# The order of a closing head group's transposes in a Mamba scan, and its reciprocal root by way of a logarithm

## The chip, the cores and the metric

One Trainium2 chip, one core. The metric is the device time of one execution in microseconds (us). The engines are PE (TensorE), DVE (VectorE), ACT (ScalarE), POOL (GpSimd) and SP (SyncE, which issues the transfers).

## The reference

Two transformer-like blocks over 256 tokens of width 1024, in fp32. The first mixes an RWKV-7 and a retention branch and a convolutional feed-forward; the second is a Mamba-2 layer, a per-layer embedding, sliding-window attention and another embedding. The change touches the Mamba-2 layer alone, whose end is a grouped norm and a product:

```python
y = ssd_chunked(xs, dt, a, bm, cm)
y = y + d_skip[:, None] * xs
y = y.reshape(b, s, D_INNER) * silu(z)
yg = y.reshape(b, s, SSM_GROUPS, D_INNER // SSM_GROUPS)          # 4 groups of 512
yg = yg * lax.rsqrt(jnp.mean(yg * yg, axis=-1, keepdims=True) + EPS)
y = yg.reshape(b, s, D_INNER) * gnorm_w
return y @ out_w
```

## The kernel before

Every engine runs one program in order, and the engines meet by semaphores. A product in fp32 precision is three TensorE products of rounded parts: an upper part, made by ACT, and a lower part (the remainder), made by DVE. Weights come in units of 1 MB; for each unit ACT makes the upper part (helper `split_to`, L1358) and DVE then the lower part (its own `split_to`, L1925). Which unit is split in which step is written out by hand (`SPLIT`).

The scan runs over 16 steps z: four head groups g, in each two chunks n of 128 tokens, in each two halves hf. For a step PE spreads the running sums of the decay (`spread`, L928, one PSUM bank of two, fed by a mask that POOL makes), ACT takes their exponentials (`exps_of`, L1723), DVE weighs them (`weigh`, L2509), and after two halves PE forms the chunk's product (`diagonal`, L440/441). At z%4==2 PE also forms the part carried over from the first chunk (`carried`, L942).

A group closes in the four steps behind it. DVE joins and gates its rows (L2534 to L2546, `gated` L2516/2518), ACT squares and sums them (`group_squares`, L1701) and takes the root (`group_root`, L1706), and at z%4==1 DVE takes the reciprocal (L2550) and scales the rows (`group_scale`, L2553). At z%4==2 PE transposes the scaled rows, four blocks for each of the two token tiles (`group_turns`, which calls `turns`, L429); both tiles go to PSUM bank 7, one after the other. ACT copies each with its norm weight (`group_upper`, L1714) and DVE makes the remainder and frees the bank (`group_lower`, L2561); on DVE the order there is lower part of tile 0, join of the group that runs (L2534, which also frees the bank for `carried`), lower part of tile 1.

Behind the waits for data, PE has one fill in each step: up to z=6 a quarter of a gate product (`z_piece`), from z=8 on a slice of the layer's output product (`out_tile`), each of twelve products (L445 to L447); z=7 has none. At z=4 and z=6 ACT also takes the Tanh of gate rows (`z_tanh`, L1659), which DVE multiplies in (`gate_rows`, L2528). Behind the scan PE goes through the rest of the output product, with group 3's transposes in between, and the embedding begins: ACT prepares a Sqrt (`root_table`, L1389), sums the squares of the rows (L1399) and takes their root, and PE transposes the scaled rows.

ACT needs a table for each function that it looks up; where another table is needed, a load (ACT_TABLE_LOAD) stands ahead of the instruction, under its line. The program does not write these loads: the build places them.

Of the kernel before, what the change touches and what calls it, by code (L numbers as in the profile page):

```python
# [24 lines left out]
ACT = mybir.ActivationFunctionType  # L25
# [132 lines left out]
def build(nc, io, out, where, ncols):  # L158
    ctx = ExitStack()
    with ctx:  # L160
# [5 lines left out]
        def sem(name):  # L166
            if name not in sems:
                sems[name] = ctx.enter_context(nc.semaphore(name))
            return sems[name]
# [22 lines left out]
        def const(name):  # L192
            a, n = where[name]
            return consts[:, a:a + n]
# [14 lines left out]
        def sm(at, *shape):  # L209
            n = int(np.prod(shape))  # L210
            v = small[:, at:at + n]
            if len(shape) == 2:
                v = v.rearrange("p (a b) -> p a b", a=shape[0])
            if len(shape) == 3:
                v = v.rearrange("p (a b c) -> p a b c", a=shape[0], b=shape[1])
            return v
# [73 lines left out]
        mean, var, rs8 = sm(8, 2, 32), sm(72, 2, 32), sm(136, 2, 32)  # L290
# [14 lines left out]
        eps6 = sm(1364, 1)  # L305
# [63 lines left out]
        def take(pe, key, bank):  # L369
            if uses[bank]:  # L370
                pe.wait_ge(psum_emptied[bank], uses[bank])
            uses[bank] += 1
            use_of[key] = (bank, uses[bank])
            return PS[bank]

        def fill(ins, key):
            ins.then_inc(psum_full[use_of[key][0]], 1)

        def full(eng, key):
            bank, n = use_of[key]  # L380
            eng.wait_ge(psum_full[bank], n)
            return PS[bank]
# [38 lines left out]
        def _(pe):  # L421
            mm = pe.matmul

            def turns(key, bank, ins):

                ps = take(pe, key, bank)
                for j, a in enumerate(ins):
                    m, n = a.shape
                    last = pe.transpose(ps[0:n, j * P:j * P + m], a, ident[0:m, 0:m])  # L429
                fill(last, key)  # L430
# [438 lines left out]
            def z_piece(j, half, i, ready=False, between=None):  # L869
                if half == 0:  # L870
                    z_banks[j, i] = take(pe, z_keys(j)[i], 2 * (j % 2) + i)
                w = unit(f"z{j}.{half}")
                for k in range(4):
                    if between and k == 2:
                        between()
                    if ready:
                        xT_ready(2, 8 * i + 4 * half + k + 1)
                    last = mm3(z_banks[j, i][:, :], both(xT, every, 4 * half + k, slice(i * P, i * P + P)),
                               both(w, every, k, every), half + k == 0, half == 1 and k == 3)
                if half:  # L880
                    fill(last, z_keys(j)[i])
                if i:
                    used(f"z{j}.{half}", *((last,) if half == 0 else (None, z_keys(j)[1])))
# [38 lines left out]
            def spread(z):  # L922

                g, n, hf = STEPS[z]
                pe.wait_ge(sem("later_steps"), z + 1)
                ps = take(pe, ("bc", z), 4 + z % 2)
                for e in range(4):
                    last = mm(ps[:, P * e:P * e + P], later[:, z % 2, e, :], const("incl"), start=True, stop=True)  # L928
                fill(last, ("bc", z))

            def diagonal(g, n):
                pe.wait_ge(sem("wT_ready"), 4 * g + 2 * n + 2)
                ps = take(pe, ("yd", g, n), 6 + n)
                for e in range(8):
                    hd = 8 * g + e
                    last = halves(ps, slice(64 * e, 64 * e + 64), wT[:, n, e, :], xd[:, n, 64 * hd:64 * hd + 64], True, True)
                fill(last, ("yd", g, n))

            def carried(g):
                emptied(pe, ("sst", g))  # L940
                ps = take(pe, ("yo", g), 6)
                fill(mm(ps[:, :], xbc[:, 20 + g, P:2 * P], ss0[:, g, :], start=True, stop=True), ("yo", g))  # L942

            def group_turns(g, i):
                pe.wait_ge(sem("yg_rows"), 2 * g + i + 1)
                turns(("gT", g, i), 7, [xs[:, i, 512 * g + P * j:512 * g + P * j + P] for j in range(4)])
# [3 lines left out]
            def out_tile(t, tiles=(0, 1)):  # L950
                g = t // 4
                w = unit(f"so{t // 2}")
                for i in tiles:
                    if t == 0:
                        for f in range(2):
                            out_banks[i, f] = take(pe, ("so", i, f), 2 * i + f)
                    pe.wait_ge(sem("ygT_ready"), 2 * g + i + 1)
                    for f in range(2):
                        last = mm3(out_banks[i, f][:, :], both(ygT[g % 2], every, t % 4, slice(i * P, i * P + P)),
                                   both(w, every, t % 2, slice(512 * f, 512 * f + 512)), t == 0, t == 15)  # L960
                        if t == 15:
                            fill(last, ("so", i, f))
                if 1 in tiles:
                    if t == 15:
                        used("so7", key=("so", 1, 1))
                    elif t % 2:
                        used(f"so{t // 2}", last)
# [22 lines left out]
            pe.wait_ge(sem("xd_ready"), 3)  # L990
            GATES = [(j, half, i) for j in (2, 3) for half in range(2) for i in range(2)][1:]
            for z, (g, n, hf) in enumerate(STEPS):
                if z % 4 == 2 and g:
                    group_turns(g - 1, 0)
                if z < 7:
                    z_piece(*GATES[z])
                if z >= 8:
                    out_tile(z - 8)
                if z % 4 == 2 and g:
                    group_turns(g - 1, 1)  # L1000
                if z + 2 < 16:
                    spread(z + 2)
                if hf:
                    diagonal(g, n)
                if z % 4 == 2:
                    carried(g)
# [324 lines left out]
        def _(act):  # L1331
# [8 lines left out]
            A = act.activation  # L1340
# [313 lines left out]
            def z_tanh(j):  # L1654


                for i in range(2):
                    ps = full(act, ("z", j, i))
                    A(zrow[:, i, 512 * j:512 * j + 512], ps[:, :], ACT.Tanh, scale=0.5).then_inc(sem("z_tanh"), 1)  # L1659
# [39 lines left out]
            def group_squares(g, i):  # L1699
                act.wait_ge(sem("yz_ready"), 2 * g + i + 1)  # L1700
                A(xd[:, i, 512 * g:512 * g + 512], xs[:, i, 512 * g:512 * g + 512], ACT.Square,  # L1701
                  accum_out=mean[:, i, g:g + 1]).then_inc(sem("yg_sq"), 1)

            def group_root(g):
                act.wait_ge(sem("yg_sq"), 2 * g + 2)
                A(var[:, :, g], mean[:, :, g], ACT.Sqrt, scale=1.0 / 512, bias=eps6).then_inc(sem("yg_root"), 1)  # L1706

            def group_upper(g, i):
                if g >= 2 and i == 0:
# [16 lines left out]
            for z, (g, n, hf) in enumerate(STEPS):  # L1726
                if z < 15:
                    exps_of(z + 1)
                if z == 4:
                    z_tanh(2)  # L1730
                if z in SPLIT:
                    split_to(SPLIT[z], -1)
                if z % 4 == 0 and g:
                    group_squares(g - 1, 0)
                if z % 4 == 1 and g:
                    group_squares(g - 1, 1)
                    group_root(g - 1)
                if z % 4 == 2 and g:
                    group_upper(g - 1, 0)
                    group_upper(g - 1, 1)  # L1740
                if z == 6:
                    z_tanh(3)
            group_squares(3, 0)
            group_squares(3, 1)
            group_root(3)
            split_to("so6", -1)
            group_upper(3, 0)
# [137 lines left out]
            for f, i, p, c in LAST:  # L1885
                z = 2 * f + i
# [8 lines left out]
        def _(ve):  # L1895
            chain = [0]

            def link(ins):
                chain[0] += 1
                ins.then_inc(sem("ve_chain"), 1)  # L1900
                ve.wait_ge(sem("ve_chain"), chain[0])
# [645 lines left out]

            def group_scale(g):
                ve.wait_ge(sem("yg_root"), g + 1)
                link(ve.reciprocal(var[:, :, g], var[:, :, g]))  # L2550
                for i in range(2):
                    c = slice(512 * g, 512 * g + 512)
                    TS(xs[:, i, c], xs[:, i, c], var[:, i, g:g + 1], None, mul).then_inc(sem("yg_rows"), 1)  # L2553
# [253 lines left out]
            for f, i, p, c in LAST:  # L2807
                z = 2 * f + i
# [27 lines left out]
```

## Time and profile before

| | us |
|---|---|
| three runs, median | 913.73 |
| lowest and highest | 911.45, 916.98 |
| the profiled execution, time | 913.91 |
| its span on the core | 912.1 |
| granted TensorE clock, mean | 0.987 |

The span is from the first to the last instruction; the 1.8 us around it belong to the execution. The profile gives busy times of each engine, the instructions in order of time, and for idle time what ended it. The scan's steps of which the text speaks lie between 645 and 725 us.

### The profile page before, as it was taken

The numbers are of one execution on the slowest core, as the hardware profiler recorded it, in microseconds if no ns is written. First come the engines' busy times: TensorE is split into PE (matmuls) and PEld (weight loads), VectorE is DVE, ScalarE is ACT, GpSimd is POOL, SyncE is SP. The second block draws the span as 40 slices with busy tenths as digits, with TensorE's granted clock in tenths as the row PEclk, the third lists the DMA queues.
The fourth block names the chain that finished last, engine by engine and source line by source line (L and its number), as shares of the span: only waits on it lengthen the run. The fifth ranks groups of instructions, "written<-read, shape, count | busy, mean of one in ns | idle before, by whom it ended". The sixth has DMA issues, their size and how long they took to land.

```text
span 912.1 us, 17764 instructions
## 1 busy us (share of the span) xinstructions
PE 865.1 (95%) x7417; PEld 740.6 (81%) x7417; DVE 650.8 (71%) x948; ACT 503.2 (55%) x722; POOL 73.4 (8%) x96
## 2 busy tenths in 40 slices
PE   5999898899999989999999899999989998999998
PEld 5997686688877789999988699987877886877777
DVE  4688427748787688888844678897776777776665
ACT  6863332334553566666534566764756666577553
POOL 6001022100000000000000000008220000000000
PEclk9999899999999989999999999999999999999999
DMA  9542242224644455566555366544223544532241
GB/s 289 186 139 93 96 123 95 96 93 139 209 183 159 161 188 185 190 201 202 194 185 185 94 189 185 186 139 139 93 93 108 181 142 162 200 108 94 93 133 53
DMA packets 80992, 136.43 MB, mean 150 GB/s; under 512 B 3957, under 2 KB 46545, under 8 KB 80912
## 3 DMA queue, kind: packets, MB, share of 16 engines
q1 hardware_dynamic: 78800, 130.76, 42.9%
q0 software_dynamic: 2112, 4.53, 1.8%
q8 instruction: 59, 0.97, 0.4%
q14 instruction: 21, 0.17, 0.1%
HBM read 134.23 MB, written 1.05 MB: 148 GB/s over the span
## 4 chain that ended last, share of the span: by engine, by line
PE 79%; DVE 7%; ACT 6%; issue 5%; DMA 2%; SPq 0%; DVEq 0%; ACTq 0%
PE bank L445 22%; PE bank L447 21%; PE bank L446 21%; PE bank L429 3%; ACT upper L1358 3%; DVE lower L1925 2%; PE bank L440 2%; PE bank L661 2%; PE bank L928 1%; PE bank L1106 1%; DVE arena L2469 1%; DMA h<-in_x 1%; ACT arena L1457 1%; DMA loaded<-in_kv_w 1%; ACT arena L1841 1%
## 5 line engine op out<-in xcount | busy, mean ns | idle before, releaser
L1925 DVE TENSOR_TENSOR lower<-loaded,upper 128x2048 fp32r<-128x2048 f32 x122 | 279.2, 2292 | 122.3 <-ACT upper L1358 120.6
L1358 ACT ACTIVATE upper<-loaded 128x2048 fp32r<-128x2048 f32 x122 | 231.9, 1904 | 117.8 <-PE bank L447 102.1
L445 PE MATMUL bank<-xT_upper,upper 128*128 128x256 f32 (+1 forms) x664 | 187.2, 282 | 1.0 <-DVE xT_lower L1990 0.9
L446 PE MATMUL bank<-xT_lower,upper 128*128 128x256 f32 (+1 forms) x664 | 185.6, 280 | 0.0
L447 PE MATMUL bank<-xT_upper,lower 128*128 128x256 f32 (+1 forms) x664 | 185.5, 279 | 0.0
L445 PE MATMUL bank<-upper,xT_upper 128*128 128x512 f32 (+1 forms) x360 | 147.7, 410 | 4.7 <-DVE lower L1925 3.5
L447 PE MATMUL bank<-upper,xT_lower 128*128 128x512 f32 (+1 forms) x360 | 140.6, 391 | 0.0
L446 PE MATMUL bank<-lower,xT_upper 128*128 128x512 f32 (+1 forms) x360 | 139.8, 388 | 0.0
L445 PEld LDWEIGHTS bank<-xT_upper,upper 128*128 128x128 f32 (+1 forms) x664 | 125.8, 190 | 2.3 <-issue 1.8
L446 PEld LDWEIGHTS bank<-xT_lower,upper 128*128 128x128 f32 (+1 forms) x664 | 126.1, 190 | 0.2
L447 PEld LDWEIGHTS bank<-xT_upper,lower 128*128 128x128 f32 (+1 forms) x664 | 126.0, 190 | 0.1
L445 PE MATMUL bank<-upper,split_arena 128*128 128x512 f32 x296 | 121.7, 411 | 3.0 <-DVE split_arena L1990 2.2
L446 PE MATMUL bank<-lower,split_arena 128*128 128x512 f32 x296 | 117.8, 398 | 0.0
L447 PE MATMUL bank<-upper,split_arena 128*128 128x512 f32 x296 | 117.6, 397 | 0.0
L445 PEld LDWEIGHTS bank<-upper,xT_upper 128*128 128x128 f32 x360 | 68.2, 189 | 21.3 <-DVE lower L1925 4.8
L447 PEld LDWEIGHTS bank<-upper,xT_lower 128*128 128x128 f32 x360 | 68.0, 189 | 14.7
L446 PEld LDWEIGHTS bank<-lower,xT_upper 128*128 128x128 f32 x360 | 68.3, 190 | 12.6 <-issue 0.5
L445 PEld LDWEIGHTS bank<-upper,split_arena 128*128 128x128 f32 x296 | 56.3, 190 | 18.2 <-DVE lower L1925 2.1
L429 PE MATMUL bank<-consts,arena 128*128 128x128 f32 (+2 forms) x333 | 50.5, 291 | 20.8 <-DMA arena<-in_norm_mix_pre 5.1
L1457 ACT ACTIVATE arena<-bank 128x512 f32<-128x512 f32 (+1 forms) x67 | 37.2, 585 | 55.4 <-PE bank L447 18.3
L447 PEld LDWEIGHTS bank<-upper,split_arena 128*128 128x128 f32 x296 | 56.1, 190 | 13.7
L446 PEld LDWEIGHTS bank<-lower,split_arena 128*128 128x128 f32 x296 | 56.3, 190 | 12.5 <-issue 0.5
(345 smaller groups left out, 1069.1 us busy)
## 6 DMA issues: line engine op xcount, KB each, us to landing
loaded<-in_w_in SPq DMA_DIRECT2D x26, 1024.0 KB, 5.1
loaded<-in_ffn_w_up SPq DMA_DIRECT2D x22, 1024.0 KB, 5.0
loaded<-in_ssm_in_w SPq DMA_DIRECT2D x20, 1024.0 KB, 5.2
loaded<-in_ffn_w_down SPq DMA_DIRECT2D x11, 1024.0 KB, 4.9
loaded<-in_ssm_out_w SPq DMA_DIRECT2D x8, 1024.0 KB, 4.8
loaded<-in_ple_gate_w SPq DMA_DIRECT2D x8, 1024.0 KB, 5.0
loaded<-in_attn_in_w SPq DMA_DIRECT2D x8, 1024.0 KB, 5.0
loaded<-in_w_branch_ret SPq DMA_DIRECT2D x4, 1024.0 KB, 4.9
```

The costliest lines, as they stand in the source:

```text
L429: last = pe.transpose(ps[0:n, j * P:j * P + m], a, ident[0:m, 0:m])
L440: mm(ps[0:64, c], a[:, 0:64], b, start=start, stop=stop)
L445: mm(out, a[0], b[0], start=start, stop=False)
L446: mm(out, a[0], b[1], start=False, stop=False)
L447: return mm(out, a[1], b[0], start=False, stop=stop)
L661: last = mm(ps[r, 32 * hd:32 * hd + 32], a[r, hd, :], b[r, hd, :], start=True, stop=True)
L928: last = mm(ps[:, P * e:P * e + P], later[:, z % 2, e, :], const("incl"), start=True, stop=True)
L1106: last = mm(ps[:, w * e:w * e + w], aqT[r, u, nh * gh * n + e, P * n:P * n + P], akT[r, u, 0:w], start=False, stop=(e == nh - 1))
L1358: A(part(upper, PARTS, n), part(loaded, LOADS, n), ACT.Copy).then_inc(uppers, 1)
L1457: empty(A(dst, ps[0:part_, 0:w], func), key)
L1841: ins = A(asb[:, z % 2, w * e:w * e + w], ps[:, w * e:w * e + w], ACT.Exp, bias=mx[:, z % 2, e:e + 1], scale=rs8[:, n, hd + e:hd + e + 1])
L1925: TT(part(lower, LOADS, n), part(loaded, LOADS, n), part(upper, PARTS, n).bitcast(F32), sub) \
```

## The change

PE's order at z%4==2 is another: both transpose sets of the closing group move behind the step's fill, and the second also behind the next spread. On ACT the root becomes Ln, a wait for it, and Exp with the factor -0.5, which gives the reciprocal root at once, so DVE's reciprocal goes. At z=6 ACT takes one Ln of a constant behind the Tanh, into a place that nobody reads.

```diff
@@ PE, the scan
             for z, (g, n, hf) in enumerate(STEPS):
-                if z % 4 == 2 and g:
-                    group_turns(g - 1, 0)
                 if z < 7:
                     z_piece(*GATES[z])
                 if z >= 8:
                     out_tile(z - 8)
                 if z % 4 == 2 and g:
-                    group_turns(g - 1, 1)
+                    group_turns(g - 1, 0)
                 if z + 2 < 16:
                     spread(z + 2)
+                if z % 4 == 2 and g:
+                    group_turns(g - 1, 1)
                 if hf:
                     diagonal(g, n)
                 if z % 4 == 2:
@@ ACT
             def group_root(g):
                 act.wait_ge(sem("yg_sq"), 2 * g + 2)
-                A(var[:, :, g], mean[:, :, g], ACT.Sqrt, scale=1.0 / 512, bias=eps6).then_inc(sem("yg_root"), 1)
+                A(var[:, :, g], mean[:, :, g], ACT.Ln, scale=1.0 / 512, bias=eps6).then_inc(sem("yg_log"), 1)
+                act.wait_ge(sem("yg_log"), g + 1)
+                A(var[:, :, g], var[:, :, g], ACT.Exp, scale=-0.5).then_inc(sem("yg_root"), 1)
@@ ACT, the scan
                 if z == 6:
                     z_tanh(3)
+                    A(sm(76, 1), eps6, ACT.Ln)
@@ DVE
             def group_scale(g):
                 ve.wait_ge(sem("yg_root"), g + 1)
-                link(ve.reciprocal(var[:, :, g], var[:, :, g]))
                 for i in range(2):
```

## Rows read from the trace of the kernel before

**Rows 1.** The page's first part: busy us, share of the span, instructions.

```profile
PE 865.1 (95%) x7417; PEld 740.6 (81%) x7417; DVE 650.8 (71%) x948; ACT 503.2 (55%) x722; POOL 73.4 (8%) x96
```

**Rows 2.** Timeline of PE: start, us, line, count, idle before and its releaser.

```profile
650.07 0.66 PE L429 MATMUL bank<-consts,arena 128*128 128x128 f32 x4
...
653.32 0.60 PE L429 MATMUL bank<-consts,arena 128*128 128x128 f32 x4
653.75 1.06 PE L928 MATMUL bank<-consts 128*128 128x128 f32 x8
...
669.70 1.12 PE L429 MATMUL bank<-consts,arena 128*128 128x128 f32 x4 [3.39 <-DVE arena L2553]
...
674.47 0.60 PE L429 MATMUL bank<-consts,arena 128*128 128x128 f32 x4
...
690.18 0.66 PE L429 MATMUL bank<-consts,arena 128*128 128x128 f32 x4
...
693.46 0.60 PE L429 MATMUL bank<-consts,arena 128*128 128x128 f32 x4
...
705.77 0.66 PE L429 MATMUL bank<-consts,arena 128*128 128x128 f32 x4 [0.73 <-DVE arena L2553]
...
723.90 1.03 PE L429 MATMUL bank<-consts,arena 128*128 128x128 f32 x8
```

**Rows 3.** Windows: length, busy of PE, PEld, DVE, ACT, POOL; PE clock; DMA.

```profile
658.00:666.00 8.00, 8.00 (x68) 6.83 (x68) 7.93 (x9) 4.44 (x8) 1.88 (x2) 1.00 0.11 10
...
669.70:673.00 3.30, 3.30 (x10) 2.82 (x11) 1.91 (x6) 1.14 (x4) 0.00 (x0) 0.51 0.00 0
```

**Rows 4.** Timeline of ACT around the root of group 0 and z=6.

```profile
646.66 1.28 ACT L1706 ACT_TABLE_LOAD   x1
647.96 0.30 ACT L1706 ACTIVATE small<-small 128x2 f32<-128x2 f32 x1
648.27 1.28 ACT L1723 ACT_TABLE_LOAD   x1
...
650.76 1.14 ACT L1714 ACTIVATE split_arena<-bank,cols 128x128 fp32r<-128x128 f32 x4 [0.60 <-PE bank L429]
...
654.97 1.11 ACT L1659 ACTIVATE arena<-bank 128x512 f32<-128x512 f32 x2
655.92 0.64 ACT L1723 ACTIVATE arena<-bank 128x512 f32<-128x512 f32 x1
656.40 1.97 ACT L1358 ACTIVATE upper<-loaded 128x2048 fp32r<-128x2048 f32 x1
```

**Rows 5.** Timeline of DVE from group 0's remainder to group 1's scale.

```profile
655.19 1.13 DVE L2561 SCALAR_TENSOR_TENSOR split_arena<-bank,cols,split_arena 128x128 fp32r<-128x128 f32 x4 [1.22 <-ACT split_arena L1714]
...
657.74 0.68 DVE L2509 TENSOR_TENSOR arena<-arena,postw 128x512 f32<-128x512 f32 x1
658.40 2.29 DVE L1925 TENSOR_TENSOR lower<-loaded,upper 128x2048 fp32r<-128x2048 f32 x1
...
665.31 2.28 DVE L1925 TENSOR_TENSOR lower<-loaded,upper 128x2048 fp32r<-128x2048 f32 x1
667.51 1.53 DVE L2509 TENSOR_TENSOR arena<-arena,postw 128x512 f32<-128x512 f32 x1
...
669.15 0.88 DVE L2553 TENSOR_SCALAR arena<-arena,small 128x512 f32<-128x512 f32 x2
```

**Rows 6.** Timeline of ACT where the layer's step sizes are formed.

```profile
580.42 0.24 ACT L1683 ACTIVATE small<-small 128x64 f32<-128x64 f32 x1
580.68 1.28 ACT L1684 ACT_TABLE_LOAD   x1
```

**Rows 7.** The chain that ended last, at the root of group 3.

```profile
702.66 0.72 ACT arena L1701 x2
703.43 1.26 issue
```

**Rows 8.** Timeline of ACT where the embedding begins.

```profile
720.40 0.19 ACT L1389 ACTIVATE small<-small 128x1 f32<-128x1 f32 x1
```

## The prediction

> **What bounds the kernel now.** The page comes first: TensorE is busy for 95% of the span [rows 1], so a change can only pay where PE stands idle or runs at a lower clock, and it costs wherever it makes PE idle. Then PE's own order of time through the scan. Its largest hole there is the 3.39 us ahead of the first transposes of group 1, which wait for DVE's scaled rows (step z=10, at 669.70); group 3 waits 0.73 us more at 705.77; groups 0 and 2 (650.07, 690.18) wait for nothing [rows 2]. After the 3.39 us the granted clock is 0.51, the lower of the two levels (1.2 instead of 2.4 GHz), for 3.30 us [rows 3]: that costs PE some 3.30 x 0.49 = 1.6 us more. So the stretch has about 3.4 + 1.6 + 0.7 = 5.7 us that a perfect edit could return. The third view is the time order of ACT and of DVE: who makes the scaled rows late. From 658 to 666 DVE is busy 7.93 of 8.00 us [rows 3]: gate rows, weights, two unit splits and the joins stand back to back from 658.40 to the scale at 669.15, and the second of these splits begins at 665.31 where group 1's gating ends [rows 5]. So at z=10 DVE is the bound, and it has no room.
>
> **Part 1, the order of the transposes.** One group has two transpose sets, both into PSUM bank 7. The second may only start when ACT has copied the first (1.14 us) and DVE has taken its remainder (1.13 us) [rows 4, 5]. From the first set to the second PE needs 653.32 - 650.07 = 3.25 us [rows 2]; at 693.46 - 690.18 it is 3.28. Today this round trip costs nothing, since a fill (twelve products) stands between the sets: 3.25 less the 0.43 of the transposes, 2.82 us, nearly its whole length. In the new order the fill goes first and only one spread of 1.06 us [rows 2] stays between. PE then idles 3.25 - 0.43 - 1.06 = 1.76 us at z=6 and z=10, and 2.82 us at z=14, where there is no spread left. Everything behind the second set (carried product, diagonal, next fill, and on ACT and DVE the copies, joins and splits queued behind the upper and the lower part) comes later by the fill's 2.8 us. The moved lines issue no DMA; the spread itself is hardly moved against the first set, so POOL's mask for the next step isn't held up.
>
> At z=6 nothing pays this back, since the first set did not wait: the second set goes from 653.32 to 656.1, the lower part of tile 1 from 655.19 to 658.0, the two Tanh of ACT from 654.97 to 657.8. At z=10 the fill now covers 2.8 us of the wait, if the scaled rows are no later than now. They are, by part 2. At z=14 the first set did not wait either: another 2.8 us.
>
> **Part 2, the root.** Today a root costs ACT a table load of 1.28 and 0.30 of Sqrt, 1.60 us from 646.66, then a second load on the way back to Exp, which stands behind the root, off the scale's path [rows 4]. The new root is Ln and then Exp, with a wait of ACT on its own Ln between (behind it stand the next step's exponentials). What it costs hangs on whether the loaded table of Ln also serves Exp. The one place where the kernel goes from Exp to Ln has a load right behind the Exp: Exp at 580.42, load at 580.68 [rows 6]. So the table that is loaded for an Exp does not serve Ln, and whoever placed that load did not look 0.4 us ahead to choose one that serves both. Nothing suggests that he looks ahead from the Ln. I take separate tables: load 1.28, Ln 0.30, load 1.28, Exp 0.25 (between the 0.19 and 0.30 of the small rows), with 0.06 between them 3.17 us, all ahead of the scale. That is 1.57 us more than now, less the reciprocal of about 0.2: +1.4 us wherever the root is on the path. The bound from below is no load at all, 0.6 us.
>
> The Trainium skill, "ScalarE: Activation LUTs", section "Table sets: the hidden batching unit", says that ln then exp is one load, since one set has both; "ScalarE activation tables: per-element evaluation and per-set limits", section "Table sets in the compiler and the runtime", says that loads are placed for the longest run. By that rule the Exp at 580.42 would already have brought Ln along; the load at 580.68 differs from it [rows 6], so the measurement decides against it here. What that rule would give is the first rival.
>
> **Part 3, the early Ln at z=6.** It stands behind both Tanh and ahead of the exponentials of step 8. With separate tables it is load 1.28, Ln 0.20, and a load 1.28 back: 2.8 us with the gaps. The exponentials go from 655.92 to 655.92 + 2.8 + 2.8 = 661.5, ACT's split behind them from 656.40 to 662.0, DVE's half of it from 658.40 to 664.0 [rows 4, 5]: +5.6 on the engine that has no room. From there to 665.31 are 6.91 us, now ending at 670.9. In this stretch DVE's weighing took 1.53 where others take 0.68, once more at 667.51 [rows 5]; I let one of the two 0.85 fall away, 670.1 (bounds 669.2 and 670.9). Squares 0.72 [rows 7], root 3.17, first scaled half 0.5 and 0.1 of passing on: first transposes at 674.6, against 669.70, **+4.9**. PE, which reached them at 666.3 and now comes 2.8 + 2.8 later, waits all the same, about 2.9 us.
>
> **The sum.** Second set of group 1 at 674.6 + 3.25, with 0.3 for a lower clock (0 to 0.5) 678.2, against 674.47: **+3.7** for everything behind it. At z=14 +2.8: **+6.5** for the second set of group 2. From there ACT and DVE carry the path (upper, split, joins, squares) to the last root at 703.43 [rows 7], which adds 1.4: group 3's transposes at 705.77 + 7.9 = 713.7. PE will have stood for some 2.5 us, and a hole of 3.39 cost 1.6 at the lower clock [rows 3]: I take half, **+0.8** (0 to 1.6). Last, the embedding's Sqrt table, which today is still there from the last root (the preparing Sqrt takes 0.19 without a load [rows 8]), must be loaded: 1.28 on ACT ahead of the row sums. PE takes up these rows at 723.90 [rows 2] without a wait; I take **+0.3** (0 to 1.28). Together 7.9 + 0.8 + 0.3 = 9.0 us. Downstream PE is nearly full, so I pass all of it on to the end. The profiled execution took 913.9 (span 912.1 and 1.8 around it), 0.2 above the median of 913.73: **922.9**.
>
> **The rivals.** (1) One table serves Ln and Exp. Then Tanh at z=6 loads one, the early Ln another: the exponentials of step 8 are as late as above. But the roots shrink to 0.6. Group 1's scale is then held by DVE alone (split and weighing behind 670.1: 672.9, rows ready 673.4), +3.7 instead of +4.9; behind the second set +2.4; with z=14 +5.2; the last root gives back 1.2, of which PE can use the 0.73 it waits today: +4.4, and 0.3 for Sqrt: **918.6** (916.5 to 920.5). For it: after that Ln the kernel next needs a Silu, so no row shows that Ln's table lacks Exp. Against: the load at 580.68. Separate tables mean that the root does not do what its form says, to spare the way back. The Trainium skill's page on the lookup tables, named above, would have it as in this rival.
> (2) It gets faster. The wait at z=10 is the place, its 3.39 + 1.6 and the 0.73 of group 3 the price: **908.1**. It decides at one point: DVE's stretch from 655 to 669 must take up the 2.8 us that the transposes lose at z=6, and ACT's loads must lie beside it. For it: the two long weighings could return up to 1.7 of that. Against: 7.93 of 8.00 busy [rows 3], and z=14 has no wait to cover.
> (3) Separate tables as forecast, but PE's holes stay short enough for the high clock and both long weighings shrink: 9.0 - 0.3 - 0.8 - 0.85 - 0.3 = 6.8, **920.7**; with all bounds the other way (0.2 + 0.8 + 0.85 + 1.0) 11.8, 925.7.
>
> **How the numbers follow.** Separate tables 0.79 (920.7 to 925.7, the likeliest at 922.9); one table 0.16; faster 0.05. The range reaches down into the second case and up by the spread of the runs shown (911.45 to 916.98): 918 to 926.5. Within 0.5% (4.6 us, about what a measurement of this kernel can tell from no change) means 909.2 to 918.3: nearly half of rival 1 and a little of the forecast, 0.11. Slower 0.84, faster 0.05.
>
> **What would show it.** Right: two table loads around each new root (four of each), two more between the Tanh and the exponentials of step 8, one ahead of the embedding's Sqrt; exponentials of step 8 near 661.5; a wait of PE of 1.7 to 2 us ahead of the second set of group 0 and 2.8 ahead of that of group 2; group 1's first set still waiting over 2 us. Wrong: no load at the new Exp (rival 1), group 1's first set without a wait, or DVE with idle time between 658 and 670 (rival 2); and the whole if the delay does not pass to the end, because a later transfer was the bound there.

## The result and the profile after

The changed kernel takes 922.39 us in the median of four runs (921.60 to 924.12), the kernel before 913.62 (911.45 to 916.98, four runs): ratio 1.0099, 95% interval 1.0074 to 1.0125. The forecast was 922.9, slower. The profiled execution has a span of 920.0 us and took 921.75.

The sequence of PE in the changed kernel shows where it stands now. The columns are start, duration, line, count, and the idle time ahead with what ended it.

```profile
652.66 0.60 PE L429 MATMUL bank<-consts,arena 128*128 128x128 f32 x4
...
655.75 0.63 PE L429 MATMUL bank<-consts,arena 128*128 128x128 f32 x4 [1.60 <-DVE split_arena L2563]
...
674.76 0.95 PE L429 MATMUL bank<-consts,arena 128*128 128x128 f32 x4 [2.46 <-DVE arena L2555]
...
678.20 1.09 PE L429 MATMUL bank<-consts,arena 128*128 128x128 f32 x4 [0.78 <-DVE split_arena L2563]
...
697.77 0.60 PE L429 MATMUL bank<-consts,arena 128*128 128x128 f32 x4
...
700.91 0.63 PE L429 MATMUL bank<-consts,arena 128*128 128x128 f32 x4 [2.55 <-DVE split_arena L2563]
...
715.09 0.66 PE L429 MATMUL bank<-consts,arena 128*128 128x128 f32 x4 [0.92 <-DVE arena L2555]
...
733.49 1.09 PE L429 MATMUL bank<-consts,arena 128*128 128x128 f32 x8
```

These are the rows that answer to [rows 2]. Two kinds of waits can be told apart by their releaser. L2555 is DVE's scale: the first set of a group waits for its rows. L2563 is DVE's lower part: the second set waits until the first has left bank 7. Before, only the first kind stood there; now the second kind stands ahead of the second set of groups 0, 1 and 2, 1.60, 0.78 and 2.55 us, and the 3.39 us at z=10 have become 2.46 and not zero.

ACT shows the root and step 8; these rows answer to [rows 4] and [rows 8].

```profile
646.40 1.28 ACT L1706 ACT_TABLE_LOAD   x1
647.69 0.30 ACT L1706 ACTIVATE small<-small 128x2 f32<-128x2 f32 x1
648.01 1.28 ACT L1708 ACT_TABLE_LOAD   x1
649.30 0.21 ACT L1708 ACTIVATE small<-small 128x2 f32<-128x2 f32 x1
...
657.43 1.10 ACT L1659 ACTIVATE arena<-bank 128x512 f32<-128x512 f32 x2
658.55 1.28 ACT L1745 ACT_TABLE_LOAD   x1
659.85 0.20 ACT L1745 ACTIVATE small<-small 128x1 f32<-128x1 f32 x1
660.06 1.28 ACT L1725 ACT_TABLE_LOAD   x1
661.35 0.60 ACT L1725 ACTIVATE arena<-bank 128x512 f32<-128x512 f32 x1
...
729.85 1.28 ACT L1389 ACT_TABLE_LOAD   x1
```

Between Ln and Exp stands a load, in each of the four roots: as this program is built, the table loaded for the Ln is not used for the Exp. The early Ln (L1745) brings two loads between the Tanh and the exponentials of step 8, where there was none before; these exponentials now start at 661.35 instead of 655.92 [rows 4]. The prepared Sqrt of the embedding (L1389) needs a load too.

DVE shows what this does to the engine that had no room (compare [rows 5]).

```profile
661.98 0.69 DVE L2512 TENSOR_TENSOR arena<-arena,postw 128x512 f32<-128x512 f32 x1 [1.70 <-ACT arena L1725]
663.78 2.29 DVE L1928 TENSOR_TENSOR lower<-loaded,upper 128x2048 fp32r<-128x2048 f32 x1 [1.11 <-ACT upper L1358]
...
670.21 2.28 DVE L1928 TENSOR_TENSOR lower<-loaded,upper 128x2048 fp32r<-128x2048 f32 x1
...
674.22 0.88 DVE L2555 TENSOR_SCALAR arena<-arena,small 128x512 f32<-128x512 f32 x2 [1.12 <-ACT small L1708]
```

It waits 1.70 us for the exponentials of step 8 and 1.11 for ACT's split, both behind the early Ln, and then 1.12 for the root. The scale starts at 674.22 instead of 669.15.

The runs differ by several us in the 645 us ahead of the scan (the same stretch begins between 643.2 and 649.8 in the profiles). So the table measures from a point inside: us from the start of the second squares of group 0 (ACT, step 5; 645.93 before, 645.66 after) to transposes of PE. The last column is the whole stretch, up to the embedding's first transposes.

| profile of | group 1 first set | group 1 second | group 2 second | group 3 first | embedding |
|---|---|---|---|---|---|
| before | 23.77 | 28.54 | 47.53 | 59.84 | 77.97 |
| changed | 29.10 | 32.54 | 55.25 | 69.43 | 87.83 |
| changed, again (e8) | 29.68 | 32.83 | 54.24 | 67.89 | 86.28 |
| order alone (e1) | 26.50 | 29.65 | 52.66 | 64.98 | 83.11 |
| root and early Ln alone (e2) | 26.82 | 31.63 | 50.87 | 64.49 | 82.88 |
| changed, no early Ln (e3) | 26.64 | 29.77 | 51.16 | 65.27 | 83.71 |
| changed, root without loads (e4) | 27.89 | 31.03 | 54.01 | 65.52 | 83.87 |
| order at z=10 alone (e5) | 23.77 | 26.91 | 45.55 | 57.86 | 76.05 |
| order at z=6, z=14 alone (e6) | 26.47 | 31.25 | 53.01 | 66.01 | 84.09 |
| half fill at z=10 (e7) | 23.76 | 26.91 | 45.52 | 57.83 | 76.02 |
| e7, later split (e9) | 22.60 | 26.07 | 44.71 | 57.01 | 75.21 |
| e9, group 3 later (e10) | 22.60 | 26.08 | 44.71 | 57.55 | 74.23 |

The stretch grew by 9.86 us. It began 0.27 earlier, and what follows it took 186.51 instead of 188.20, so the span grew by 7.9: 9.86 - 0.27 - 1.69. The 1.69 are the clock. Before, PE runs a spell of 4.70 us in the embedding at 0.66, which costs 4.70 x 0.34 = 1.6 us; in the changed kernel the same spell has the full clock. The windows view (length, busy time of each engine, granted clock, DMA), of before and then of the changed kernel:

```profile
765.30:770.00 4.70, 4.68 (x14) 3.73 (x15) 4.07 (x8) 2.41 (x5) 0.00 (x0) 0.66 0.01 3
```

```profile
775.00:779.70 4.70, 4.70 (x20) 3.83 (x21) 4.05 (x8) 3.86 (x5) 0.00 (x0) 1.00 0.11 15
```

### The profile page after: what moved, and what is told of

It is laid out like the page before. It is cut to its first block, busy times and chain, and to the rows that moved or that the text cites. A ratio compares the mean times of both kernels' runs of the same rounds, so it can differ in the third digit from the quotient of the medians.

```text
span 920.0 us, 17769 instructions
## 1 busy us (share of the span) xinstructions
PE 867.6 (94%) x7417; PEld 740.3 (80%) x7417; DVE 648.5 (70%) x944; ACT 509.2 (55%) x731; POOL 72.6 (8%) x96
## 4 chain that ended last, share of the span: by engine, by line
PE 77%; ACT 8%; DVE 7%; issue 5%; DMA 2%; SPq 0%; DVEq 0%; ACTq 0%
PE bank L445 22%; PE bank L447 20%; PE bank L446 20%; PE bank L429 3%; ACT upper L1358 2%; PE bank L440 2%; DVE lower L1928 2%; PE bank L661 2%; PE bank L928 1%; PE bank L1106 1%; DVE arena L2472 1%; ACT arena L1457 1%; DMA h<-in_x 1%; DMA loaded<-in_kv_w 1%; ACT arena L1844 1%
## 5 line engine op out<-in xcount | busy, mean ns | idle before, releaser
L429 PEld LDWEIGHTS bank<-consts,arena 128*128 128x128 f32 (+2 forms) x333 | 40.7, 148 | 33.8 <-issue 13.4
```

## The experiments

The theory: the second set's round trip through bank 7 loses its cover at z=6 and z=14, and two tables make every root and the early Ln longer; the two parts add up. The rivals: all of it is the root; the order by itself gains; ACT had time for the loads.

### Each part alone

```diff
e1_order: the changed kernel with its new order, and
-                A(var[:, :, g], mean[:, :, g], ACT.Ln, scale=1.0 / 512, bias=eps6).then_inc(sem("yg_log"), 1)
-                act.wait_ge(sem("yg_log"), g + 1)
-                A(var[:, :, g], var[:, :, g], ACT.Exp, scale=-0.5).then_inc(sem("yg_root"), 1)
+                A(var[:, :, g], mean[:, :, g], ACT.Sqrt, scale=1.0 / 512, bias=eps6).then_inc(sem("yg_root"), 1)
...
-                    A(sm(76, 1), eps6, ACT.Ln)
...
+                link(ve.reciprocal(var[:, :, g], var[:, :, g]))
```

> Only the new order of the transposes; the root is Sqrt and reciprocal as before, with no early Ln. My theory (the second set's round trip through bank 7 is no longer covered): group 0's second set 2.8 us later at z=6, group 1's first set near 671.6 with next to no wait of PE ahead of it, group 2's second set again 2.8 later; behind the scan +3.5, so 917.3 us (916 to 919). The rival that the order by itself gains (the 3.4 us wait at z=10 and its 1.6 of lower clock go away, the rest is hidden) expects 908 to 911.

Measured: 916.94 us, ratio 1.0028 (1.0007 to 1.0048). The order alone is slower, so the rival by which it gains has fallen. Its rows:

```profile
656.66 0.60 PE L429 MATMUL bank<-consts,arena 128*128 128x128 f32 x4
659.75 0.63 PE L429 MATMUL bank<-consts,arena 128*128 128x128 f32 x4 [1.59 <-DVE split_arena L2561]
...
676.16 0.66 PE L429 MATMUL bank<-consts,arena 128*128 128x128 f32 x4 [0.45 <-DVE arena L2553]
679.31 0.63 PE L429 MATMUL bank<-consts,arena 128*128 128x128 f32 x4 [1.59 <-DVE split_arena L2561]
...
702.32 0.63 PE L429 MATMUL bank<-consts,arena 128*128 128x128 f32 x4 [2.54 <-DVE split_arena L2561]
```

The wait at z=10 shrinks from 3.39 to 0.45, as the edit means it to. But 1.59 us of waiting for bank 7 appear at z=6 and z=10 and 2.54 at z=14. The stretch is 5.14 longer, 1.6 more than expected; a spell at the lower clock behind the last 1.59 accounts for this:

```profile
680.00:684.00 4.00, 3.79 (x8) 2.37 (x9) 2.29 (x7) 3.40 (x6) 0.00 (x0) 0.57 0.02 6
```

At 0.57 these 4.00 us cost 1.7. The kernel before has such a spell too, between the two sets of z=10 [rows 3]; here it stands behind them.

```diff
e2_root: the kernel before, and
-                A(var[:, :, g], mean[:, :, g], ACT.Sqrt, scale=1.0 / 512, bias=eps6).then_inc(sem("yg_root"), 1)
+                A(var[:, :, g], mean[:, :, g], ACT.Ln, scale=1.0 / 512, bias=eps6).then_inc(sem("yg_log"), 1)
+                act.wait_ge(sem("yg_log"), g + 1)
+                A(var[:, :, g], var[:, :, g], ACT.Exp, scale=-0.5).then_inc(sem("yg_root"), 1)
...
                     z_tanh(3)
+                    A(sm(76, 1), eps6, ACT.Ln)
...
-                link(ve.reciprocal(var[:, :, g], var[:, :, g]))
```

> Only the new root with the early Ln; the order of the transposes as before. My theory (two loads at every root, two more at z=6): exponentials of step 8 about 3 us later, group 1's first set near 672.7, PE idle about 6 us ahead of it at z=10, group 3's set +4.5, an extra load at the embedding: 918.8 us (917 to 921). The rival that the whole loss comes from the root and the order is neutral expects 922.

Measured: 916.67 us, ratio 1.0034 (1.0011 to 1.0058), 2 us under the forecast and just under its range; the rival's 922 is far off. In the profiled execution what follows the stretch took 186.52 us, as in the changed kernel, without the 1.7 of the spell in the embedding. In the profile the step comes out as expected: first set of group 1 at 26.82, that is 672.75 on the time of before, group 3 +4.65, stretch +4.91. PE's hole at z=10 grows to 5.43 us:

```profile
671.72 1.11 PE L429 MATMUL bank<-consts,arena 128*128 128x128 f32 x4 [5.43 <-DVE arena L2555]
```

In the stretch the parts add up: 5.14 + 4.91 = 10.05 against 9.86 for both. By the medians it is 0.28% + 0.34% against 0.99% here and 0.72% in a second comparison (e8 below); the intervals are too wide to say more.

### The early Ln, and the loads of the roots

```diff
e3_no_early_ln: the changed kernel, and
-                    A(sm(76, 1), eps6, ACT.Ln)
```

> The changed kernel without the early Ln at z=6. My theory (its two loads delay the exponentials of step 8 and so the unit split on DVE, which has no room): exponentials of step 8 near 658.6 instead of 661.35, group 1's first set about 2.4 us earlier than in the changed kernel, 919.8 us (918.5 to 921). The rival that ACT has time for it and nothing moves expects 922.4.

Measured: 918.38 us, ratio 1.0045 (1.0027 to 1.0064), just under the forecast's range. The exponentials follow the Tanh at once:

```profile
655.24 1.10 ACT L1659 ACTIVATE arena<-bank 128x512 f32<-128x512 f32 x2
656.20 0.63 ACT L1725 ACTIVATE arena<-bank 128x512 f32<-128x512 f32 x1
```

The Tanh starts where it did in the changed kernel (11.76 us from the mark against 11.77), the exponentials 12.72 instead of 15.69. Group 1's first set comes 2.46 us earlier (26.64 against 29.10; 2.4 were expected), the stretch is 4.1 shorter than in the changed kernel and 2.6 shorter than in its second profile. So the instruction, by its place one meant to bring a table early, costs 2.5 us or more of the stretch, on the path.

```diff
e4_root_no_loads: the changed kernel, and
-                A(var[:, :, g], mean[:, :, g], ACT.Ln, scale=1.0 / 512, bias=eps6).then_inc(sem("yg_log"), 1)
+                A(var[:, :, g], mean[:, :, g], ACT.Identity, scale=1.0 / 512, bias=eps6).then_inc(sem("yg_log"), 1)
...
-                A(var[:, :, g], var[:, :, g], ACT.Exp, scale=-0.5).then_inc(sem("yg_root"), 1)
+                A(var[:, :, g], var[:, :, g], ACT.Identity, scale=-0.5).then_inc(sem("yg_root"), 1)
```

> The changed kernel with Identity in the place of Ln and of Exp in the four roots, so that the rows are scaled by another factor, but the two instructions, their wait and the early Ln stay and the roots need no table. This stands for one table that serves both. My theory: group 1's first set held by DVE alone near 673.4, the last root 1.2 us shorter than before, 918.6 us (917 to 920). The rival that the roots' loads lie beside the path expects 922.4.

Measured: 918.77 us, ratio 1.0054 (1.0034 to 1.0075); forecast 918.6. The root is two short instructions:

```profile
668.65 0.30 ACT L1706 ACTIVATE small<-small 128x2 f32<-128x2 f32 x1
668.98 0.21 ACT L1708 ACTIVATE small<-small 128x2 f32<-128x2 f32 x1
```

It ends 2.6 us sooner than with two loads, yet group 1's first set gains only 1.2 to 1.8 (27.89 against 29.10 and 29.68): from there DVE is the bound. Group 3's set gains 2.4 to 3.9. So, as far as this stand-in goes, the change would have been slower than before even if one table had served both, at about rival 1's sum (918.6).

### Where the order loses and where it gains

```diff
e5_order_z10: the kernel before, the new order only at z=10
-                if z % 4 == 2 and g:
+                if z in (6, 14):
                     group_turns(g - 1, 0)
...
-                if z % 4 == 2 and g:
+                if z in (6, 14):
                     group_turns(g - 1, 1)
+                if z in (10,):
+                    group_turns(g - 1, 0)
                 if z + 2 < 16:
                     spread(z + 2)
+                if z in (10,):
+                    group_turns(g - 1, 1)
```

> The old root; the new order at z=10 only, the old one at z=6 and z=14. My theory (at z=10 the fill covers DVE's lateness, and the second set's own wait of 1.6 to 1.8 us eats part of it): first set of group 1 without a wait of over 0.7 us, second set about 1.5 us earlier than before; from the scan's step 5 to the embedding's transposes 76 to 78 us against 78.0 before, so 912 to 914 us; if the shorter holes also bring the lower clock, no gain at all. The rival that this place is where the new order loses expects 916 or more.

Measured: 910.17 us, ratio 0.9966 (0.9945 to 0.9986). Better than expected, and faster than before:

```profile
667.66 0.66 PE L429 MATMUL bank<-consts,arena 128*128 128x128 f32 x4 [0.40 <-DVE arena L2557]
670.80 0.63 PE L429 MATMUL bank<-consts,arena 128*128 128x128 f32 x4 [1.59 <-DVE split_arena L2565]
```

```profile
671.00:690.00 19.00, 18.73 (x150) 15.21 (x148) 14.84 (x24) 12.26 (x21) 1.61 (x1) 1.00 0.30 112
```

One hole of 3.39 us has become two of 0.40 and 1.59, and the clock stays at 1.00. The stretch is 1.92 shorter.

The table says where these 1.92 us come from. The first set of group 1 comes no earlier than before (23.77 in both), since DVE makes its rows no sooner. The second follows it after 3.14 us instead of 4.77. At the full clock the old order needs no more than 3.25 and 3.28 (z=6 and z=14 of the kernel before), so, as an estimate from these rows, about 1.5 us are the lower clock behind the hole of 3.39, which doesn't come here, and the order by itself returns only the rest, some 0.4. The same kernel once more, beside the last two below:

> The order at z=10 only, again, beside the two above: 76.05 us to the embedding's transposes and about 3 us below the kernel before, if the gain is one of the order and not of that chip.

It gave 910.58 us and 0.9984 (0.9963 to 1.0005), with 75.97 us for the stretch: the stretch repeats, the gain in the whole is somewhere between nothing and 0.5%. The runs' clocks point the same way: the mean granted clock is 0.9904 in e5 against 0.9886 of the kernel before beside it, and 0.9924 against 0.9894 in e11. Times the span, that is an estimated 1.7 and 2.8 us less that the clock takes, where the mean times differ by 3.5 and 1.9; how much of it lay on the path in each execution is not shown.

```diff
e6_order_z6_z14: as e5, with (10,) and (6, 14) exchanged
```

> The old root; the new order at z=6 and z=14 only, the old one at z=10. My theory (both places lose the fill's 2.8 us with nothing to pay for it, and at z=10 PE still waits, for rows that come 2 us later): 82 to 83.5 us from step 5 to the embedding's transposes against 78.0 before, 917 to 918.5 us. The rival that the loss lies at z=10 expects 914.

Measured: 919.25 us, ratio 1.0066 (1.0040 to 1.0092), stretch +6.12, a little over the forecast. So the order loses at z=6 and z=14, where the first set did not wait, and gains at z=10, where it did and the clock fell behind the wait. PE still waits 3.40 us at z=10, and the clock falls behind this and behind z=14 (the first window takes in most of the hole; from the set's start, 672.00 to 675.30, it is 0.51 as before):

```profile
670.00:675.50 5.50, 3.50 (x11) 2.98 (x12) 4.03 (x9) 3.09 (x7) 0.80 (x1) 0.69 0.17 70
698.00:703.00 5.00, 4.19 (x11) 2.64 (x12) 3.03 (x8) 2.94 (x5) 0.00 (x0) 0.66 0.01 3
```

e5 and e6 give -1.92 + 6.12 = 4.20 for the stretch, where the order as a whole gives 5.14 with a spell at the lower clock that e5 does not have.

### The changed kernel again

> The changed kernel once more, beside the three above on one chip, to set the parts against the whole. My theory: 922.4 us, and 87.8 us from step 5 to the embedding's transposes, as the sum of the order alone (+5.1) and the root alone (+4.9) on 78.0 says. If the parts do not add up, it is nearer to 918.

Measured: 920.93 us, ratio 1.0072 (1.0043 to 1.0100), beside e5 to e7 on one chip. The stretch is 86.28, 1.55 shorter than in the first profile of the very same program. The waits are about as long or longer:

```profile
675.14 0.66 PE L429 MATMUL bank<-consts,arena 128*128 128x128 f32 x4 [2.42 <-DVE arena L2555]
678.29 0.63 PE L429 MATMUL bank<-consts,arena 128*128 128x128 f32 x4 [1.59 <-DVE split_arena L2563]
```

But the clock behind them is full, where the first profile had 0.53, and 0.71 behind group 2's. The windows behind the holes of z=6 and behind the first set of group 1, of this profile:

```profile
655.50:660.00 4.50, 4.18 (x28) 3.30 (x30) 3.03 (x7) 3.76 (x9) 0.62 (x1) 0.71 0.32 130
...
675.00:679.00 4.00, 2.18 (x16) 1.78 (x16) 2.86 (x8) 1.24 (x6) 1.04 (x1) 1.00 0.00 0
```

and of the first profile, behind that set and behind group 2's second:

```profile
674.70:679.50 4.80, 3.96 (x17) 3.51 (x18) 2.81 (x8) 1.32 (x5) 1.04 (x1) 0.53 0.00 0
...
700.80:704.40 3.60, 3.21 (x9) 2.04 (x10) 1.81 (x5) 2.82 (x5) 0.00 (x0) 0.71 0.02 5
```

The windows cut the spells short. In the first profile the lower clock lies between 674.5 and 682.0 (0.54 over 7.50 us, which is at most 7.50 x 0.46 = 3.4 us of slower work) and between 702.0 and 706.0 (0.57 over 4.00, 1.7 us). In the second, within the stretch, it lies between 657.0 and 661.0 alone (0.57 over 4.00, 1.7 us), where PE has its wait at z=10 still ahead. The first set of group 1 is 0.58 later there (29.68 against 29.10), but not by this spell: up to 23.1 us behind the mark DVE runs alike in both profiles, and then one of its instructions takes 1.41 instead of 0.69 us. From the first profile and from the second:

```profile
669.60 0.69 DVE L2519 TENSOR_TENSOR arena<-arena 128x512 f32<-128x512 f32 x1
```

```profile
669.27 1.41 DVE L2519 TENSOR_TENSOR arena<-arena 128x512 f32<-128x512 f32 x1
```

So the change costs the stretch 86.28 - 77.97 = 8.31 us where the spell falls ahead of a wait, and 9.86 where up to 5.1 us of slower work fall behind the waits. Both are counted from a profile of before that has one spell of its own.

### A version that beats both

```diff
e7_half_fill: the kernel before, and at z=10
-                if z % 4 == 2 and g:
+                if z % 4 == 2 and g and z != 10:
                     group_turns(g - 1, 0)
...
-                if z >= 8:
+                if z == 10:
+                    out_tile(2, (0,))
+                    group_turns(1, 0)
+                    out_tile(2, (1,))
+                elif z >= 8:
                     out_tile(z - 8)
...
                     spread(z + 2)
+                if z == 10:
+                    group_turns(1, 1)
```

> The old root and order, but at z=10 half of the fill (six products) ahead of the first set, the other half and the spread ahead of the second. My theory (the hole of 3.4 us falls into two of under 2 us, and the clock stays up): second set about 1.6 us earlier than before, 75.5 to 76.5 us from step 5 to the embedding's transposes against 78.0, 911.5 to 912.5 us. The rival that DVE sets the pace from there anyway expects 913.7, as before.

Measured: 911.65 us, ratio 0.9980 (0.9953 to 1.0008), stretch 76.02: the profile is as forecast, the time alone is not clear of the runs' spread. As in e5 the first set has not moved (23.76) and the clock stays up, so here too the gain is mostly the clock's.

```diff
e9_half_fill_late_split: as e7, and on DVE
-                if z in SPLIT:
+                if z in SPLIT and z != 8:
                     split_to(SPLIT[z], -1)
...
                     join_diagonal(g, 0)
+                    if z == 10:
+                        split_to(SPLIT[8], -1)
```

> The kernel of the half fill at z=10 with one thing more: DVE's half of the unit split of step 8 moves behind the join of step 10. My theory (what holds group 1's first set is DVE's stretch of splits and joins, so one split less ahead of the scale brings it forward until ACT's root holds it): first set of group 1 about 1.1 us earlier, 22.6 us behind step 5's squares instead of 23.8, the second set as much, 74.9 us to the embedding's transposes against 76.0; about 910.5 us. The rival that the split only moves the delay to the second remainder expects 76.0 and no gain on the half fill.

Measured: 909.18 us, ratio 0.9969 (0.9948 to 0.9990). The first set comes at 22.60, as forecast, which confirms that DVE's stretch held it; now DVE waits 1.80 us for ACT's root ahead of the scale. The second gains 0.84 and the stretch 0.81 (1.1 were expected): part of the split's time now stands ahead of the second remainder.

```diff
e10_late_split_and_tail: as e9, and behind the scan
             for t in range(8, 12):
-                out_tile(t)
-                if t == 9:
+                out_tile(t, (0,))
+                if t == 10:
                     group_turns(3, 0)
+                out_tile(t, (1,))
```

> As the one before, and group 3's first transposes half a fill later, behind the first half of the third output slice. My theory: the wait of 0.7 us ahead of them goes, nothing behind needs them sooner; 74.2 us to the embedding's transposes, about 909.8 us. The rival that their remainder is then late for the last output slices expects 75 or more.

Measured: 909.74 us, ratio 0.9966 (0.9940 to 0.9992), stretch 74.23 as forecast, 3.74 under the kernel before; the wait of 0.71 ahead of group 3 is gone. In time it can't be told from e9 and e5; all three lie 2 to 4 us under the kernel before, in whose profiled stretch some 1.5 us are the lower clock. In none of their profiles, nor in e7's, does the clock fall in the stretch.

## Why the prediction was right

**The bound.** That DVE held group 1's first set was right: one split less ahead of the scale brought it forward by 1.16 us (e9). In the changed kernel it is ACT's root that the scale waits for (1.12 us at 674.22), as part 3's sum has it.

**Part 1.** The round trip of 3.25 us and its cover were right. Waits of 1.76, 1.76 and 2.82 us were forecast ahead of the second sets; in e8 they are 1.59, 1.59 and 2.55: the round trip takes 3.08 to 3.15 there, and at z=14, with no spread behind them, 0.60 of it are the transposes, not 0.43. That z=10 alone gains, and z=6 and z=14 lose, is shown by e5 and e6; that the gain at z=10 is mostly the clock, the prediction does not say.

**Part 2.** Separate tables were taken at 0.79, from the one load between an Exp and an Ln [rows 6]. The rows after bear it out: 646.40 to 649.51 are 3.11 us, forecast 3.17. What the Trainium skill says in "ScalarE: Activation LUTs", section "Table sets: the hidden batching unit", that ln then exp is one load, does not hold for this program: each of the four roots has a load ahead of either function (646.40 and 648.01 in the first). e4 stands in for the case that it holds: 918.8, still above the kernel before.

**Part 3.** The exponentials of step 8 were forecast for 661.5 and came at 661.35, DVE's split 664.0 and 663.78, the first set 674.6 and 674.76. e3 shows that these two loads were on the path. Two slips did no harm. PE's wait of about 2.9 us is 2.7 by the prediction's own times (674.6 - 666.3 - 5.6), and was 2.46. And one of its signs of being wrong did show, DVE idle between 658 and 670 (1.70 and 1.11 us). The sign was badly chosen: exponentials at 661.5 and the split at 664.0, as forecast, leave DVE without work there, so it does not speak for the rival that expected a gain.

**The sum.** Second set of group 1: +3.7 forecast, +4.0 measured in the table's terms. Second set of group 2: +6.5 and +7.7. Group 3: +7.9 and +9.6. Embedding: +0.3 for the Sqrt load, and 9.86 - 9.59 = 0.27. The term that was mis-sized is the lower clock. The prediction put 0.3 behind group 1 and 0.8 behind group 3's hole. In the first profile the clock fell behind group 1's and group 2's sets (0.53 and 0.71), and not at all behind group 3's:

```profile
713.50:718.00 4.50, 3.58 (x18) 2.65 (x18) 2.53 (x3) 4.49 (x8) 0.00 (x0) 1.00 0.64 206
```

So the place was wrong, and the amount comes and goes: the stretch was 9.86 longer with the spells behind the waits and 8.31 with one ahead of a wait, 9.0 was forecast. The waits themselves were summed up well. In e8, whose one spell doesn't delay the next set, the same places come +4.3, +6.7 and +8.1 later, and the embedding 8.31 in all, against a forecast of 7.9 + 0.3 = 8.2 without the 0.8 for the clock. The step that all of it passes on to the end was right in e8 (188.26 us behind the stretch, 188.20 before, with a like spell in the embedding: 0.57 over 773.0 to 777.0) and 1.7 too much in the first profile, by the spell that fell away there. So it is in part luck that the median came within 0.5 us of 922.9: in the first profile a stretch longer than forecast and an embedding faster than forecast offset each other, and in e8 the same program is 0.72% slower than before (0.43 to 1.00) where 1.0% was forecast.

**What stays open.** Why a hole is followed by the lower clock in one execution and not in another was not tried; the program of the two profiles of the changed kernel is the same, and up to the first spell, behind z=6 in e8, the one long wait is 1.60 us in one and 1.59 in the other. Nor was one table for Ln and Exp itself run, only roots that need none.

## What to carry to other kernels

A fill placed between two uses of one buffer pays for the round trip of that buffer: before it is moved ahead to cover another wait, look, place by place, whether that other wait is there at all. Here it was at one of three places, and moving the fill only there turned a loss into a gain. What it gained there was for the most part not the wait, which moved from the first set to the second, but the granted clock, which fell behind one hole of 3.39 us and not behind two of 0.40 and 1.59; so look at the clock behind a hole before crediting the order. A function pair that replaces one function has to be priced by the table loads in the trace, and an instruction that is meant to bring a table early is itself two loads on an engine that runs in order if the next function needs another table.

## What the runs showed of the hardware that was not expected

The lower clock costs as much as one of the edits here, and comes and goes in the same program: behind holes of 2.46 and 2.42 us ahead of the same transposes the granted clock was 0.53 over 4.80 us in one profile and 1.00 over 4.00 us in the other. A spell in the stretch was worth up to 1.7 us of slower work (0.57 over 4.00 us in e1 and e8) or twice that (0.54 over 7.50 us in the changed kernel's first profile). A hole of 3.39 or 3.40 us was followed by the same 0.51 over the 3.30 us behind it (before; e6 from 672.00 to 675.30); with the hole split into 0.40 and 1.59 (e5, and again 0.39 and 1.59 in e11) the clock stayed at 1.00. In e1, though, holes of 0.45 and 1.59 were followed by 0.57.
